# Index scores after every quarter of a token tile, slab lower parts on VectorE, and two feature tiles moved into the attention loop of a two-layer hybrid decoder step

## What is computed

```python
u = rms_norm(x, p['g_pre_mix'])
(q, k, v, qi, ki, wi, bx, gb, gc, glu, zg, xbc, dt) = jnp.split(u @ p['w_in'], cuts, axis=-1)
...
def select_keys(qi, wi, ki, qpos, topk):
    s = jnp.einsum('bqhd,bsd->bqhs', qi, ki) * IDX_DIM ** -0.5
    score = jnp.einsum('bqhs,bqh->bqs', jax.nn.relu(s), wi * N_IDX_HEADS ** -0.5)
    score = jnp.where(kpos[None, None, :] <= qpos[None, :, None], score, -jnp.inf)
    _, idx = lax.top_k(score, topk)
```

## Time and profile before

| | us |
|---|---|
| median of 3 runs | 1466.51 |
| lowest, highest | 1465.22, 1470.06 |
| the profiled execution, its own time | 1465.05 |
| its span, first to last instruction | 1463.3 |
| mean granted TensorE clock | 0.964 of full speed |
| TensorE matmuls busy | 1368.9 (94%) |
| VectorE busy | 1017.8 (70%) |
| ScalarE busy | 652.4 (45%) |
| GpSimd busy | 184.2 (13%) |

### The profile page before, as it was taken

How to read it: one execution, slowest core, us unless ns; L and a number is a source line. 1 busy time by engine, 2 the same in 40 slices (tenths; PEclk the granted TensorE clock), 3 DMA queues, 4 the chain that set the end, 5 groups by cost and what they waited for, 6 DMA issues and landing times.

```text
span 1463.3 us, 29326 instructions
## 1 busy us (share of the span) xinstructions
PE 1368.9 (94%) x11014; PEld 1267.0 (87%) x11014; DVE 1017.8 (70%) x2141; ACT 652.4 (45%) x1202; POOL 184.2 (13%) x132
## 2 busy tenths in 40 slices
PE   5999979997999999999879998899979999999997
PEld 5789865787999999999767997648979999999996
DVE  5489898744899999322366898987259999982223
ACT  4443335444556666322244422445344665653222
POOL 0334312021000000001030442121100000000000
PEclk9999989998999999999979999999989999999998
DMA  7443231221523333433254333212223233335321
GB/s 267 123 126 101 66 94 61 93 72 44 159 73 108 107 101 101 155 91 98 95 165 127 100 84 94 66 69 82 88 81 108 88 114 102 100 97 160 88 88 59
DMA packets 223892, 149.85 MB, mean 102 GB/s; under 512 B 13650, under 2 KB 218810, under 8 KB 222758
## 3 DMA queue, kind: packets, MB, share of 16 engines
q1 hardware_dynamic: 221174, 141.09, 32.4%
q0 software_dynamic: 2624, 7.48, 1.4%
HBM read 128.92 MB, written 16.03 MB: 99 GB/s over the span
## 4 chain that ended last, share of the span: by engine, by line
PE 80%; DVE 14%; ACT 3%; issue 2%; SPq 1%; DMA 0%; POOL 0%; DVEq 0%; ACTq 0%
PE PS L684 29%; PE PS L1149 24%; PE PS L785 11%; PE PS L756 2%; PE PS L757 2%; PE PS L758 2%; PE PS L912 1%; DVE side L2016 1%; DVE x L2281 1%; PE PS L663 1%; PE PS L700 1%; PE PS L739 1%; PE PS L740 1%; PE PS L741 1%; DVE arena L1768 1%
## 5 line engine op out<-in xcount | busy, mean ns | idle before, releaser
L1149 PE MATMUL PS<-b_hi,a_hi 128*128 128x260 f32 x1008 | 286.2, 284 | 3.0 <-DVE last_lo L2364 2.2
L1149 PE MATMUL PS<-b_lo,a_hi 128*128 128x260 f32 x1008 | 284.4, 282 | 0.0
L2169 DVE TENSOR_TENSOR w_lo<-ring,w_hi 128x640 fp32r<-128x640 f32 (+2 forms) x88 | 87.5, 995 | 242.4 <-ACT w_hi L1403 242.1
L1149 PEld LDWEIGHTS PS<-b_hi,a_hi 128*128 128x128 f32 x1008 | 189.9, 188 | 4.5 <-DVE last_lo L2364 2.7
L1149 PEld LDWEIGHTS PS<-b_lo,a_hi 128*128 128x128 f32 x1008 | 190.3, 189 | 0.0
L1403 ACT CAST w_hi<-ring 128x1024 fp32r<-128x1024 f32 (+2 forms) x92 | 80.1, 871 | 234.3 <-PE PS L684 234.3
L785 PE MATMUL PS<-u_hi,w_hi 128*128 128x260 f32 x576 | 123.4, 296 | 13.6 <-ACT hid L1345 13.6
L684 PE MATMUL PS<-hid_hi,w_lo 128*128 128x260 f32 x656 | 132.3, 283 | 0.0
L684 PE MATMUL PS<-hid_hi,w_hi 128*128 128x260 f32 x656 | 132.1, 283 | 0.0
L684 PE MATMUL PS<-hid_lo,w_hi 128*128 128x260 f32 x656 | 131.9, 283 | 0.0
L1149 PE MATMUL PS<-b_hi,s_lo 128*128 128x260 f32 x432 | 122.1, 283 | 0.0
(11 more groups left out here) (401 smaller groups left out, 3329.1 us busy)
## 6 DMA issues: line engine op xcount, KB each, us to landing
ring<-in_ffn_gate SPq DMA_DIRECT2D x44, 512.0 KB, 3.7
ring<-in_ffn_up SPq DMA_DIRECT2D x44, 512.0 KB, 3.7
ring<-in_w_in SPq DMA_DIRECT2D x36, 512.0 KB, 3.6
ring<-in_ffn_down SPq DMA_DIRECT2D x32, 384.0 KB, 3.4
ring<-in_ffn_down SPq DMA_DIRECT2D x32, 320.0 KB, 3.0
x_store<-x SPq DMA_DIRECT2D x4, 2080.0 KB
x<-x_store SPq DMA_DIRECT2D x4, 2080.0 KB, 8.3
ring<-in_w_out SPq DMA_DIRECT2D x16, 512.0 KB, 4.2
```

Of the source, the lines that this page charges most:

```text
L1149: ins = pe.matmul(bank(ACC[up][to])[:, 0:HALF], w[:, k, :], b[:, k, :], start=(start and k == 0 and w is whi and b is bhi), stop=(k == KC ...
L2169: dve.tensor_tensor(w_lo[part % 2][:, 0:n, :], raw[part % 4][:, 0:n, :], w_hi[part % 2][:, 0:n, :].bitcast(F32), ALU.subtract).then_inc(pa ...
```

## The change

- Slabs 1 and 2 get their lower parts on VectorE (one function `slab_lower` for all slabs), issued right behind the normalisation; all of their upper casts on ScalarE come together, ahead of the copies of slab 0's tiles.
- The list `TOK_TILES` moves tile (1, 0) ahead of slab 0's sample tile (0, 4). The turn of qi and ki follows the first quarter (two of eight k chunks) of (0, 4). Index products follow every quarter of a tile, three at a time, from the end of (0, 4) on, at eight places instead of six.
- `SPREAD_FROM` goes from 7 to 5, `LOOP_TILES` thereby from 11 to 9, and `STEP_PRODUCTS` takes 336 products instead of 240 in its two halves per step. The samples' lower rows on GpSimd (`rows_lo`) follow tile 5 instead of tile 6.
- On VectorE the first two operations on dt go from ahead of the index scores to ahead of top-k, and the rotation of k and of the samples' rows from round 4 to round 8.

```diff
-        SPREAD_FROM = 7
+        SPREAD_FROM = 5
...
-        STEP_PRODUCTS = (14, 12, 13, 9, 13, 9, 13, 9, 13, 9, 9)
+        STEP_PRODUCTS = (18, 16, 17, 13, 17, 14, 17, 14, 17, 13, 12)
...
-        IDX_PLACES = [(1, 1, 1), (1, 2, 0), (1, 2, 1), (1, 3, 0), (1, 3, 1), (1, 4, 0)]
-        IDX_AT = {place: range(4 * i, 4 * i + 4) for i, place in enumerate(IDX_PLACES)}
+        TOK_TILES = [(0, t) for t in range(QT)] + [(1, 0), (0, QT)] + [(1, t) for t in range(1, QT + 1)] +             [(2, t) for t in range(QT + 1)]
+        TURN_QI = (0, QT, 0)
+        IDX_PLACES = [(0, QT, 3)] + [(1, 1, q) for q in range(4)] + [(1, 2, q) for q in range(3)]
+        IDX_AT = {place: range(3 * i, 3 * i + 3) for i, place in enumerate(IDX_PLACES)}
...
# TensorE
+                        pe.wait_ge(*past(layer, tok_ready, g - 1 if g > QT + 1 else g - QT + 1))
...
+                            if k % 2:
+                                if (s, t, k // 2) == TURN_QI:
+                                    pe.wait_ge(*past(layer, rope_done, 2))
+                                    pe.wait_ge(*past(layer, tok_ready, QT))
+                                    turn(tok_qi, 0, bank(4))
+                                    turn(tok_qi, 1, bank(5))
+                                    turn(ki_four, 0, bank(6))
+                                idx_products((s, t, k // 2))
...
# ScalarE
-                    slab_upper(1, 0)
+                    for s in range(1, N_TOK):
+                        for i in range(len(tok_pieces[s])):
+                            slab_upper(s, i)
...
-                            if s == 0 and t < 2:
-                                slab_upper(2, t)
...
+                    for g, (s, t) in enumerate(TOK_TILES):
+                        for place in range(3):
+                            idx_rectified((s, t, place))
+                            if (s, t, place) == TURN_QI:
                                 for j in range(3):
                                     turned_out(j, 4 + j, 4 + j)
...
+                        idx_rectified((s, t, 3))
...
# VectorE
+                    for s in range(1, N_TOK):
+                        for i in range(len(tok_pieces[s])):
+                            slab_lower(s, i)
                     dve.memset(tap_col[96:P], 0.0).then_inc(tap_cols_ready, 1)
...
-                    dve.wait_ge(*past(layer, tok_ready, QT + 1))
-                    dve.wait_ge(*past(layer, states_ready, 4))
-                    step(dve.tensor_tensor(per_head(dt_v), per_head(dt_v), head_all[:, 0:1, :].broadcast_to(blocks), ALU.add))
...
                     dve.wait_ge(*past(layer, rope_done, 3))
+                    dve.wait_ge(*past(layer, tok_ready, QT + 2))
+                    dve.wait_ge(*past(layer, states_ready, 4))
+                    step(dve.tensor_tensor(per_head(dt_v), per_head(dt_v), head_all[:, 0:1, :].broadcast_to(blocks), ALU.add))
...
                     for r in range(TOPK_PROMPT // 8):
-                        if r == 4:
+                        if r == 8:
                             rope_tiles(tok_k, HEADS, HD, 16, tab, 2 * (QT + 1) + QT).then_inc(rope_done, 1)
...
# GpSimd
-                    for s in range(1, N_TOK):
-                        for i in range(len(tok_pieces[s])):
-                            slab_lower(s, i)
...
-                        if f == 6:
+                        if f == SPREAD_FROM:
                             pool.wait_ge(*past(layer, rows_hi_ready, 3))
```

More of the change, by code:

```diff
@@ L363, in hybrid_decoder @@
         x_kept, x_back = sem("x_kept", 32), sem("x_back", 32)
-        first_lo = x8_turned
-        per_layer[first_lo.num] = 2
-        slab_hi, slab_lo = sem("slab_hi", 5), sem("slab_lo", 3)
+        slab_hi, slab_lo = sem("slab_hi", 5), sem("slab_lo", 5)
         tile_in = [sem(f"tile_in{i}", 64 if i < 2 else 80) for i in range(4)]
@@ L728, in _ @@
                               .then_inc(states_turned, 1)
[L729 to L770, removed]
@@ new lines, in _ @@
+                        m = P if t < QT else NS
+                        to = bank(tok_bank(g))[0:m, 0:tok_w[s]]
+                        pe.wait_ge(*past(layer, tok_ready, g - 1 if g > QT + 1 else g - QT + 1))
+                        for k in range(KC):
+                            if t == 0 and k in [a for a, _, _, _ in tok_pieces[s]]:
+                                pe.wait_ge(*past(layer, slab_lo, sum(len(p) for p in tok_pieces[:s]) +
+                                           [a for a, _, _, _ in tok_pieces[s]].index(k) + 1))
+                            u_k, lo_k = u_hi[:, k, t * P:t * P + m], m_lo[k][:, t * P:t * P + m]
+                            hi, lo = tok_k_of(tw_hi, s, k), tok_k_of(tw_lo, s, k)
+                            pe.matmul(to, u_k, hi, start=(k == 0), stop=False)
+                            pe.matmul(to, u_k, lo, start=False, stop=False)
+                            last = pe.matmul(to, lo_k, hi, start=False, stop=(k == KC - 1))
+                            if k == KC - 1:
+                                last.then_inc(tok_summed, 1)
+                            if k % 2:
[6 more added lines that the diff above has]
+                                idx_products((s, t, k // 2))
@@ L2525, in tile_lower @@
                                            ALU.subtract).then_inc(tile_lo, 1)
-                    def slab_lower(s, i):
-                        pool.wait_ge(*past(layer, slab_hi, sum(len(p) for p in tok_pieces[:s]) + i + 1))
-                        pool.tensor_tensor(tw_lo[s][i][:, :, :], slab_raw[s][i][:, :, :], tw_hi[s][i][:, :, :].bitcast(F32),
-                                           ALU.subtract).then_inc(slab_lo, 1)
-                    for s in range(1, N_TOK):
-                        for i in range(len(tok_pieces[s])):
-                            slab_lower(s, i)
                     tile_lower(0)
```

86 lines of the change are left out of this document (46 added, 40 removed).

## The result

The changed kernel took **1480.47 us**, median of 4 runs (1479.84 to 1481.88), against 1466.51 before: a ratio of 1.0093, 95% interval 1.008 to 1.0106. It is 14 us slower where 1459.7 was forecast, and outside the range of 1448.0 to 1468.5. The profiled execution took 1480.32 us, 15.3 more than that of before.

What follows compares the result with a forecast made beforehand. TensorE was taken to bound the kernel up to the attention loop, then VectorE, then very nearly TensorE from step 6. Starting 11.3 us earlier less 7.9 of loop growth gives 3.4 per layer, 6.8 for two: 1459.7 us, range 1448 to 1468.5.

Steps and rivals of the forecast that it cites:

- What bounds the kernel: TensorE up to the attention loop; inside it VectorE first, then from step 6 TensorE very nearly sets the pace.
- The slabs' lower parts and the index scores: Ahead of the spread loop: 7.0 us of lower parts hidden in VectorE's idle time; first sample done 10.7 us earlier.
- The index groups: Token products: two more groups break the tile products, costing between nothing and the 0.62 us won; taken as 0.
- Two tiles less ahead: Ahead of the spread loop: 96 products fewer, 11.5 us; with a 0.2 us wait, attention loop starts 11.3 us earlier.
- The growth of the loop by 7.9 us: Attention loop: 5.8 us for 48 products behind step 6, 1.7 for one more end of tile, 0.4 for GpSimd's hold.
- the granted clock under 0.7 between steps 6 and 11: Attention loop: listed sign in the new profile that the forecast is wrong; TensorE's clock staying reduced there.
- the last rival: Attention loop, pauses in steps 6 and 9: two half-clock stretches cost 8.4 us per layer, 1476.5 us; chance 0.08.
- VectorE's hold by GpSimd: Attention loop, steps 0 to 5: one more GpSimd lower part holds VectorE from nothing to 2.2 us; taken as 0.4.
- The sum: Whole kernel: 11.3 - 7.9 = 3.4 us won per layer, 6.8 for two; median 1459.7 us.

Runs made afterwards that it cites:

- the front part alone: Changed kernel with SPREAD_FROM back at 7 and the old table of 240 products, keeping early index scores and slabs' lower parts on VectorE: 1472.6 us, ratio 1.0031.
- both together, with repaired pauses: Changed kernel with ScalarE's copy ahead of the cast, more products in steps 0 to 5 (two tables tried), and pauses filled with useless products: 1452.9 us each.
- the loop part alone: Kernel before with only SPREAD_FROM 5 (five tiles ahead of the spread loop) and the new table of 336 products: 1501.9 us, ratio 1.0233.

## Why the prediction was wrong

**What bounds the kernel**: right. TensorE very nearly set the pace behind step 6, and with more work there VectorE waited in steps 8 and 11, the two places named, and 2.14 us in step 10.

**The slabs' lower parts and the index scores**: right. 6.70 us for 7.0, hidden; first rotation 0.42; first index product at 51.56, first addition at 52.71 for 52.9, first max at 75.1 for 74, the third spread not waiting. Some of this is luck: from the first max to the masks it took 55.6 us where 58.2 was forecast, and the masks took 2.66 where 0.9 was, which nearly cancels. The index groups were put at nothing net; the token products took 1.0 us more per layer although the wait of 0.62 went. The eight groups themselves take 7.0 us where the six took 5.8, and the two more breaks some 0.2 each.

**Two tiles less ahead**: 10.3 for 11.3. The index groups are most of the difference, and a lower part of GpSimd that came late cost a wait of 0.21 at 111.47.

**The growth of the loop by 7.9 us is the step that failed.** It was worked out for full clock: the forecast put the loss to half clock at nothing. With the pauses filled the growth was 7.8; as the kernel ran, it was 13.4. The 5.6 between them is the clock. That 7.8 meets 7.9 is partly luck, for one of the terms was too small as well: the ends of tiles behind step 6 cost 3.2 us more than before, not 1.7, and 0.5 of idle time and 0.8 that VectorE was ahead made up for it. The end of a tile was taken as 1.7 us wherever it falls, and the new table puts one behind the exponential of step 9, which stands behind two table loads. ScalarE's timeline of the changed kernel:

```profile
212.92 1.28 ACT L1375 ACT_TABLE_LOAD   x1
214.21 0.24 ACT L1375 ACTIVATE side<-side 128x48 f32<-128x48 f32 x1
214.47 1.28 ACT L1415 ACT_TABLE_LOAD   x1
215.77 0.61 ACT L1415 ACTIVATE arena<-arena,small 128x384 f32<-128x384 f32 x1
...
216.38 1.03 ACT L1286 CAST w_hi<-ring 128x1024 fp32r<-128x1024 f32 x1
217.31 0.59 ACT L1336 ACTIVATE hid<-PS 128x520 f32<-128x520 f32 x1
```

Such loads of 1.28 us stood in the trace of before too, at 218.47 and 220.03, but behind the old end of a tile in step 8. Now they made a pause of 3.18 where 1.69 was counted. The Trainium skill ("ScalarE: Activation LUTs", section "What ACT_TABLE_LOAD costs") gives 1283 ns for the load, and the trace agrees (1.28); it adds a drain of about 1380 ns to each switch, which the trace doesn't show, as the next operation begins 0.01 us behind the load.

The half clock itself was not unforeseen. The prediction held it for a rival, priced two stretches in the loop at 8.4 us per layer (1476.5) and gave that a chance of 0.08; against the half clock behind step 6 it had that the trace showed it in one layer only. In both layers of the changed kernel the clock fell at the long pauses (the granted clock under 0.7 between steps 6 and 11 that the prediction named as its refutation), and a fourth stretch, behind the state rows, hadn't been thought of: TensorE came to step 12 at full clock and waited 3.28 us there, where before it was at half clock (232 to 239) and waited 0.94. Three in the loop cost 5.8 us in the first layer and the fourth 5.0, together 10.8 where two had been priced at 8.4. So it was the last rival that came true in its mechanism. That its 1476.5 is near 1480.5 is partly luck: it counted on two stretches of 10 us, and there were three of 3.2, 3.5 and 6.0 in the loop and one of 10 behind it.

**VectorE's hold by GpSimd** (0.4 us): not seen on balance. The long operations fell elsewhere (six small ones at 182.33 took 3.32 us where they had taken 1.25, but one that had taken 2.45 at 191.74 took 0.29), and VectorE was 0.8 us faster to step 7 than before.

**The sum** comes out nearly for a kernel whose clock stays up: 1461.2 measured with these pauses filled, for 1459.7. But filling also takes away half clock that the old kernel had. Like for like, both filled, the change is worth 3.9 us (1465.1 against 1461.2) where 6.8 was forecast; 2.0 of the difference are the start of the loop, 10.3 us earlier instead of 11.3 in each layer.

## What to carry to other kernels

Work that is moved onto an engine's idle time is cheap only if it leaves the pauses that remain short: price TensorE's work next to every pause at full and at half clock, and look which engine sets the pace behind it. Where TensorE does, shorten the pause first (copy out of PSUM before starting the next cast; let no tile end behind an operation that waits for a slower engine or a table load), and then fill it with products into an unused half of a bank. And an earlier start of one stage need not give anything by itself: here the front part alone cost 4.7 us and the moved tiles alone 34, while both together, with repaired pauses, gained 15.

## What the runs showed of the hardware

- Filling 72 products per layer into pauses of 1.7 and 3.2 us made a kernel 0.8% faster (1480.5 to 1468.9), 26 more in one pause another 0.5% (1461.2), with TensorE busy for 93 to 95% of the span either way. The mean granted clock (0.959 in the changed kernel, 0.976 in the last) shows little of this: what counts is where the missing share lies.
- At three pauses of 3.18 to 3.28 us in the first layer's loop the granted clock fell to 0.50, during the pause or within 2 us behind it, and so it did at one of 1.69 us (204.9 to 206.6), not long behind another such stretch. Where these four were filled there was none. Pauses of 1.69 alone, in steps 2 and 4, were not followed by one. The length of the pause doesn't decide alone: one of 3.18 us in the run with the loop part alone and one of 2.98 in the kernel before had full clock behind them, while with the pauses filled the clock still fell at 232, where the only pause near was 1.22 us. What else decides wasn't measured.
- The Trainium skill ("TensorE: Matmul & The Clock Gate", section "HAM oscillation — how this bites in real kernels") has waits between bursts of products throw TensorE back each time. The runs with filled pauses agree, for a kernel that is busy for nine tenths of the time; but here not each time, as the two pauses just named show.
- That the slabs' lower parts moved to VectorE pay by themselves wasn't tried apart from the rest; the trace shows only that they were hidden.
